# The last convolution tap taken from PSUM, and TensorE's wait for the qk product one level later, in a hybrid DeltaNet and short-convolution block

## What is computed

```python
xn = rms_norm(h, norm1)
proj = xn @ w_in
q, k, v, z, b_raw, a_raw, sc_c, sc_u, sc_b, gate_a, gate_b = split_columns(proj, PROJ_WIDTHS)
qkv = silu(causal_depthwise_conv(concatenate([q, k, v]), conv_qkv))      # 4 taps per channel
...
o = chunk_gated_delta_rule(q, k, v, g, beta)                             # 8 heads, chunks of 64
o = rms_norm(o, o_norm) * silu(z);  y_a = o @ w_dn_out
y_b = (sc_b * causal_depthwise_conv(sc_c * sc_u, conv_sc)) @ w_sc_out    # 3 taps per channel
mixed = sigmoid(gate_a) * y_a + sigmoid(gate_b) * y_b
h = h + mixed @ w_o
gt, up = split(rms_norm(h, norm2) @ w_gate_up);  h = h + (silu(gt) * up) @ w_down
```

## Time and profile before

| | us |
|---|---|
| median of 3 runs | 1152.71 |
| lowest and highest run | 1152.14, 1153.82 |
| span of the profiled execution, first to last instruction | 1150.6 |
| TensorE busy | 1109.3 (96%) |
| GpSimd, ScalarE, VectorE busy | 561.0, 452.3, 436.0 |

### The profile page before, as it was taken

How to read it: one execution, slowest core, us unless ns; L and a number is a source line. 1 busy time by engine, 2 the same in 40 slices (tenths; PEclk the granted TensorE clock), 3 DMA queues, 4 the chain that set the end, 5 groups by cost and what they waited for, 6 DMA issues and landing times.

```text
span 1150.6 us, 20455 instructions
## 1 busy us (share of the span) xinstructions
PE 1109.3 (96%) x8363; PEld 940.9 (82%) x8363; DVE 436.0 (38%) x651; ACT 452.3 (39%) x961; POOL 561.0 (49%) x502
## 2 busy tenths in 40 slices
PE   7999899898989899898999999999999999999996
PEld 6999799897979799896878888878888888888884
DVE  6465847566575847565110011222112111100002
ACT  5554546362644546363332232434222333222221
POOL 4363535335353535335344455674555555554552
PEclk9999999998999999998999999999999999999998
DMA  4221111121211111111152323222223332223321
GB/s 172 75 68 63 56 57 56 58 69 49 68 56 57 56 56 57 56 64 53 69 168 95 103 80 104 92 92 92 92 92 94 101 99 92 92 92 96 100 79 73
DMA packets 26621, 93.27 MB, mean 81 GB/s; under 512 B 2849, under 2 KB 3105, under 8 KB 26529
## 3 DMA queue, kind: packets, MB, share of 16 engines
q1 hardware_dynamic: 25488, 89.88, 23.6%
q10 hardware_dynamic: 1040, 2.10, 0.5%
HBM read 89.87 MB, written 2.10 MB: 80 GB/s over the span
## 4 chain that ended last, share of the span: by engine, by line
PE 82%; DVE 9%; ACT 5%; issue 4%; POOL 1%; DVEq 0%; ACTq 0%; POOLq 0%
PE bank L1050 82%; DVE cv L940 4%; DVE am L759 1%; DVE xt L759 1%; ACT L730 1%; ACT w_hi L495 1%; DVE xd L927 0%; ACT xd L499 0%; DVE qkv L774 0%; DVE raw L759 0%; DVE h L1043 0%; POOL w_lo L389 0%; DVE vb L759 0%; ACT nwt L605 0%; ACT am L499 0%
## 5 line engine op out<-in xcount | busy, mean ns | idle before, releaser
L389 POOL TENSOR_TENSOR w_lo<-w_raw,w_hi 128x512 fp32r<-128x512 f32 x324 | 416.9, 1304 | 542.9 <-ACT w_hi L495 542.6
L1050 PE MATMUL bank<-x_hi,w_hi 128*128 128x264 f32 (+1 forms) x896 | 253.9, 342 | 4.3 <-DVE x_lo L778 3.6
L1050 PE MATMUL bank<-x_lo,w_hi 128*128 128x264 f32 (+1 forms) x896 | 235.4, 322 | 0.0
L1050 PE MATMUL bank<-x_hi,w_lo 128*128 128x264 f32 (+1 forms) x896 | 234.3, 320 | 0.0
L495 ACT ACTIVATE w_hi<-w_raw 128x512 fp32r<-128x512 f32 x324 | 187.7, 622 | 107.0 <-PE bank L1050 106.7
L1050 PEld LDWEIGHTS bank<-x_hi,w_hi 128*128 128x128 f32 x896 | 150.9, 194 | 19.8 <-issue 3.4
L1050 PE MATMUL bank<-og_hi,w_hi 128*128 128x512 f32 x416 | 164.7, 396 | 0.0
L1050 PE MATMUL bank<-og_hi,w_lo 128*128 128x512 f32 x416 | 164.3, 395 | 0.0
L1050 PE MATMUL bank<-og_lo,w_hi 128*128 128x512 f32 x416 | 164.3, 395 | 0.0
L1050 PEld LDWEIGHTS bank<-x_hi,w_lo 128*128 128x128 f32 x896 | 151.0, 193 | 11.5
L1050 PEld LDWEIGHTS bank<-x_lo,w_hi 128*128 128x128 f32 x896 | 151.9, 194 | 8.7
(11 more groups left out here) (253 smaller groups left out, 1379.2 us busy)
## 6 DMA issues: line engine op xcount, KB each, us to landing
w_raw<-w_stream SPq DMA_DIRECT2D x162, 512.0 KB, 3.3
h_in<-h_t SPq DMA_DIRECT2D x4, 528.0 KB, 5.0
h<-h_t ACTq DMA_DIRECT2D x1, 2048.0 KB, 9.9
out<-h SPq DMA_DIRECT2D x8, 256.0 KB, 2.1
cst<-consts SPq DMA_DIRECT2D x1, 512.0 KB, 8.1
sm<-small SPq DMA_DIRECT2D x1, 80.5 KB, 6.1
wba<-w_ba SPq DMA_DIRECT2D x1, 64.0 KB, 7.3
```

Of the source, the lines that this page charges most:

```text
L389: nc.gpsimd.tensor_tensor(w_lo[:, n % 2, at], w_raw[:, n % 3, at], w_hi[:, n % 2, at].bitcast(f32), ALU.subtract).then_inc(wlo_ready, 1)
L1050: return nc.tensor.matmul(o, w, x, start=start, stop=stop)
```

## The change

For q, k and v, ScalarE now writes the last tap into cv, as a copy out of PSUM with the tap's weight as factor, ahead of the copy into raw. VectorE adds the remaining three taps; the pass that only multiplied is gone. For u, VectorE itself writes the last tap, (PSUM x weight) x cbuf, in two halves, and adds two taps instead of doing three. The waits that protect the cv buffer move to whoever writes it first. On TensorE the wait for qkt_ready moves from level 0 to level 1, in front of the first write into dbank[3].

```diff
 # ScalarE, evacuate of q, k, v
                         act.wait_ge(zeroed, 1)
+                        act.wait_ge(xlo_ready, KT // 2)
+                        act.wait_ge(xlo_even, KT // 2)
+                    if kind == "k" and m:
+
+                        act.wait_ge(yb_ready, m)
+                    if kind == "q" and m:
+                        act.wait_ge(qkv_ready, 3 * m)
+                    if kind == "v":
+                        act.wait_ge(qkv_ready, 3 * m + 1)
+                    last = CQKV + 4 * (8 * ("q", "k", "v").index(kind) + m) + 3
+                    for s in range(2):
+                        nc.scalar.activation(cv[:, c % 2, s * HALF:(s + 1) * HALF], p[s][:, 0:HALF], ACT.Copy,
+                                             scale=sm[:, last:last + 1])
                     copy(raw[:, c % 2, 3:3 + HALF], p[0][:, 0:HALF])
                     copy(raw[:, c % 2, 3 + HALF:3 + L], p[1][:, 0:HALF]).then_inc(raw_ready, 1)
 # VectorE, convolve
-                n = taps.shape[1]
+                n = taps.shape[1] - 1
                 for j in range(n):
                     xj = x[:, first_column + j:first_column + j + L]
-                    if j == 0:
-                        ins = nc.vector.tensor_scalar(to, xj, taps[:, 0:1], None, ALU.mult)
-                    else:
-                        ins = nc.vector.scalar_tensor_tensor(to, xj, taps[:, j:j + 1], to, ALU.mult, ALU.add)
+                    ins = nc.vector.scalar_tensor_tensor(to, xj, taps[:, j:j + 1], to, ALU.mult, ALU.add)
 # VectorE, evacuate of q, k, v
-                    if c < 2:
-                        dve.wait_ge(xlo_ready, KT // 2)
-                        dve.wait_ge(xlo_even, KT // 2)
-                    elif kind != "k":
-                        dve.wait_ge(qkv_ready, 3 * m + (i > 0))
 # VectorE, evacuate of u
+                    dve.wait_ge(qkv_ready, 3 * m + 2)
+                    last = CSC + 3 * m + 2
+                    halves = (slice(0, HALF), slice(HALF, L))
+                    for s, half in enumerate(halves):
+                        nc.vector.scalar_tensor_tensor(cv[:, c % 2, half], p[s][:, 0:HALF], sm[:, last:last + 1],
+                                                       cbuf[:, half], ALU.mult, ALU.mult)
                     mult(raw[:, c % 2, 3:3 + HALF], p[0][:, 0:HALF], cbuf[:, 0:HALF])
                     mult(raw[:, c % 2, 3 + HALF:3 + L], p[1][:, 0:HALF], cbuf[:, HALF:L]).then_inc(c_used, 1)
                     dve.wait_ge(c_used, m + 1)
                     yield
-                    dve.wait_ge(qkv_ready, 3 * m + 2)
 # TensorE, delta step 4, 6, ...
                                 pe.wait_ge(mkv_ready, h + 1)
-                                pe.wait_ge(qkt_ready, h + 1)
...
+                            if l == 1:
+                                pe.wait_ge(qkt_ready, h + 1)
                             if 1 <= l < META_LEVELS:
                                 mm(dbank[3][0:META, 256:264], mpb[:, l - 1, :], cols(mt[:, :], LEVELS[l - 1], 0))
```

## The result

The change takes the median from 1152.43 us (four runs of the kernel before on the same chip) to 1137.99 us (four runs, 1133.80 to 1139.70). The ratio is 0.9867, with a 95% interval of 0.9856 to 0.9879: faster by 1.3%. The prediction was 1140.6 us. The profiled execution took 1139.7 us, the longest of the four, and its span is 1137.9 us, against 1150.6 us before, so 12.7 us less.

What follows compares the result with a forecast made beforehand. TensorE, busy 96%, was taken as the bound, losing 35.9 us to waits and clock. With 16.5 us waiting and 7.3 us clock left, the gain is 12.1: 1152.7 - 12.1 = 1140.6 us, own range 1133 to 1147, overall 1114 to 1148.

Steps and rivals of the forecast that it cites:

- What can be won (35.9 us): TensorE's seven waits for xt plus the lower clock after them, 4.74 or 5.63 us each: at most 35.9 us.
- rival A: u's first tap gets its turn after one GpSimd instruction; TensorE waits nowhere, all 35.9 us go: 1116.8 us, chance 0.26.
- The held tap: u's first tap on VectorE stays held until GpSimd is idle, ending 0.57 us later; main case, chance 0.61.
- The wait (2.36 us): TensorE waits 2.36 us per head for um's update instead of 3.29 for xt; 16.5 us over seven.
- The clock: After TensorE's waits, five of seven are followed by a clock fall of 1.45 us each: 7.3 us.
- ScalarE's pair for q, k and v: Two factored copies per block take 0.7 us against 0.81 us cover in the k block; nothing charged.
- VectorE's pair for u: Two scalar_tensor_tensor from PSUM ahead of the raw mults take 0.84 us of 1.14 us cover; no charge.
- Rival C: VectorE's new instructions from PSUM for u are held too; 27 us more, 1180 us, chance 0.05.
- Rival B: Nothing moves: longer-held tap, ScalarE's added copies or um's transpose take what the wait gives; 1152 us, chance 0.08.
- The signs: Held tap: seven um waits about 2.4 us, u's first tap about 5 us, heads 62 to 63.5, head 0 59.6.
- The guess about the prelude: GpSimd's 16x16 instructions (mt, malev), followed by more work without a pause, cause VectorE's tap to be held; no size given.

Runs made afterwards that it cites:

- experiment 1: Kernel before with only TensorE's wait for qkt_ready moved from level 0 to level 1: 1141.94 us, ratio 0.9926.
- experiment 2: Kernel before with the moved qkt_ready wait and the last tap from PSUM for u alone; q, k and v unchanged: 1139.20 us, ratio 0.9887.
- 9: Changed kernel with a GpSimd pause ahead of the three 16x16 malev instructions: 1140.33 us, ratio 0.9887.
- experiment 11: Changed kernel with a GpSimd wait behind malev on a semaphore that already has its value (a_ready), so no pause: 1139.58 us, ratio 0.9873.
- experiment 3: Changed kernel with TensorE's wait for qkt_ready put back to level 0: 1153.38 us, ratio 1.0005.
- Experiments 4: Changed kernel with GpSimd waiting for the end of its own last malev instruction (mt_ready) before w_lo: 1116.75 us, ratio 0.9691.
- 7: Kernel before, with none of the change, plus GpSimd's wait for mt_ready before w_lo: 1116.34 us, ratio 0.9690.
- experiment 10: Changed kernel, no pause added, with GpSimd's five instructions on ma, mt and malev made 128x16 instead of 16x16: 1116.69 us, ratio 0.9682.
- experiment 12: Changed kernel with GpSimd waiting for its own instruction behind the second alev, while the tap is already held: 1116.63 us, ratio 0.9681.
- experiment 5: Changed kernel with GpSimd's wait for mt_ready behind malev, plus one 16x16 scratch multiplication between that wait and w_lo: 1121.64 us, ratio 0.9740.

## Why the prediction was right, and where it was off

**What can be won (35.9 us).** Right. The kernels in which the tap gets its turn stand at 1116.3 to 1116.8 us; rival A had 1116.8.

**The held tap.** Right, and by the rows it rested on: the tap ends 0.57 us after GpSimd's last alev, as the last tap of v did after dg_lo. The step taken from head 0, that the instruction gets its turn, would have been wrong by 21 us.

**The wait (2.36 us).** 2.20. The chain was right, and one stretch of the sum was too big by 0.14 us. GpSimd is idle at 202.75 where I had 203.19, and TensorE ready at 205.11 - 2.20 = 202.91 where I had 203.33: both are earlier by about the same, and that cancels. What remains is the step from the tap's end to the level's start, 205.11 - 203.32 = 1.79 us, for which I had worked out 205.69 - 203.76 = 1.93. Most of it is TensorE's start 0.05 us after um's update ends (205.06), for which I had taken the 0.15 seen behind xt; the last tap takes 0.68 us to the update's start and not 0.74.

**The clock (five of seven fall, 1.45 each, 7.3 us).** Four fell, three of 1.43 us and the last of 2.8, 7.1 us together. That the sum came so near is luck: one fall fewer than I let happen, and one twice as dear. The number was a choice, and it does not hold still: of the six stretches between the seven waits of a profiled run, those with a fall were three in the change, three in experiment 1, five in 2, three in 9 and four in 11, all with waits of 2.2 to 2.7 us. Behind waits of 3.29 us (before) and 3.56 us (experiment 3) it was six of six. The change's spread of 5.9 us between runs fits this: the slowest run has falls for 7.1 us, and the mean granted clock of the four runs, from the fastest to the slowest, is 0.994, 0.990, 0.988 and 0.987. Only the slowest has a trace. The kernels without waits spread by 0.2 to 0.9 us.

**ScalarE's pair for q, k and v (0.7 us against a cover of 0.81).** The pair takes 0.72 us from its start to that of the raw copies, as forecast, and the cover was needed. The k block of head 4, ScalarE and then TensorE:

```profile
283.48 0.82 ACT L668 ACTIVATE cv<-bank,sm 128x264 f32<-128x264 f32 x2
284.20 0.63 ACT L495 ACTIVATE raw<-bank 128x264 f32<-128x264 f32 x2
...
286.70 0.36 ACT L495 ACTIVATE nwt<-bank 64x256 f32<-64x256 f32 x1
```

```profile
287.35 0.48 PE L1060 MATMUL bank<-wba,mkdec 16*128 16x128 f32 x2
```

By itself a factored copy of this size takes longer than a plain one (465 ns by the mean against 378), but the second starts before the first has ended. The level's product is copied by 287.06 and TensorE takes it at 287.35: of the 0.81 us 0.29 are left, more than the 0.11 forecast, mostly because the pair starts sooner behind the 16x128 copy ahead of it (283.48 - 283.30 = 0.18 us after that one's start, where the raw copies of before started after 288.54 - 288.20 = 0.34). No wait came of it, so the charge of nothing stands. By these numbers (an estimate) two more copies there would have been late.

**VectorE's pair for u (0.84 us against 1.14).** 0.87 us together. TensorE reads um at 198.34, and the transpose has ended at 198.08: 0.26 us are left of the cover. Right.

**Rival C** (the new instructions from PSUM are held too): the pair took 0.87 us while GpSimd was in alev and mt. It did not happen. **Rival B** (nothing moves) did not either: both covers held, with 0.29 and 0.26 us left, and the wait fell to 2.20 us. **The signs** named ahead came as for the held tap: heads of 61.9 to 63.3 us, a first tap of 5.32 us, and head 0 at 59.64.

**The guess about the prelude** was that GpSimd's 16x16 instructions without a pause behind them bring the hold. Experiments 4, 7, 9, 10, 11 and 12 bear it out. The fifth shows that it was too simple: a single one behind a pause did it in one head of seven.

The Trainium skill, "SBUF — State Buffer", section "Who interferes with whom", has the loser blocked for the whole of one instruction of the other engine. Where GpSimd's work in this place is on 128 partitions the taps agree with it: they end 0.57 us after the one instruction that runs when they are asked for (experiment 10). Behind work on 16 partitions without a pause the hold lasts six instructions (5.32 us in the change), and the measurement decides.

**Not settled.** What in GpSimd the 16 partitions change is not shown by any row; the profile has one row per instruction and nothing of its parts. That they leave GpSimd's work out of step, so that nothing is free between two of its instructions, is a guess that would fit the counts of 0, 1 and 7 and the cure by a pause; no run tests it. Why one 16x16 instruction behind a pause holds one head in seven, and one with no pause ahead (mdg) holds seven in seven, was not tried apart.

## What to carry to other kernels

When an instruction takes several times what its form takes elsewhere, and always ends the same short time after another engine falls idle, ask what releases it before moving its reader: the change goes round a stall that one wait on GpSimd removes (1116.34 us on the kernel before, as low as any that was run). Look for instructions on few partitions (16 here) ahead of an unbroken run of GpSimd work, and either give them all 128 or let GpSimd wait for its own last one. Test a change that hides part of a stall against the removal of the stall alone.

## What the runs showed of the hardware that was not expected

- GpSimd instructions on 16 partitions, in a row with later ones, kept a VectorE instruction out for six GpSimd instructions: a scalar_tensor_tensor on two tensors in SBUF (5.3 to 5.6 us), and a TENSOR_SCALAR on one and a factor too (5.8 us). The same on 128 partitions, for one (0.75 to 1.77 us, the scalar_tensor_tensor alone was tried). They take no longer themselves: 0.21 us and 0.22 us.
- A pause of 0.08 us in GpSimd ends it, also when VectorE is already held (experiment 12). A wait whose semaphore has its value makes no pause (experiment 11).
- With identical times to a hundredth of a microsecond, one head of seven was held and six were not (experiment 5).
- A gap of 2.2 to 2.7 us in TensorE's work was followed by a fall of the clock in 18 of 30 head stretches, of 3.29 or 3.56 us in 12 of 12. It cost about 1.43 us each time, but for two heads of the kernel before (2.34 us), one of experiment 2 (2.7) and the change's seventh wait (2.8), which is not among the 30.
